# Gate projection with the frames' tiles standing and 24 weight columns moving, and moved products, loads and orders, in a hybrid GLA, mLSTM and ConvFFN step

## The reference, cut to what matters

```python
h = _rmsnorm(x, norm1)
gq, gk, gv, gr, glr, mq, mk, mv, mo, mi, mf = _split_proj(h @ w_in)
log_a = jax.nn.log_sigmoid((glr @ w_gla_a + b_gla_a).astype(f32)) / GLA_TAU
i_pre = mi.astype(f32) + b_m_i.astype(f32)
log_f = jax.nn.log_sigmoid(mf.astype(f32) + b_m_f.astype(f32))
o_g, S_new = _gla(...)          # gq, gk, gv, log_a;  gated by gr
h_m, C_new, n_new, m_new = _mlstm(...)   # mq, mk, mv, i_pre, log_f;  gated by mo
x = x + mix.astype(x.dtype) @ w_out
y, conv_new = _conv_ffn(_rmsnorm(x, norm2), conv_st, w_g, w_u, conv_w, conv_b, w_d)
```

## Time and profile before

| | us |
|---|---|
| median of 3 runs | 1443.26 (1441.57 to 1443.32) |
| profiled execution | 1442.54 |
| its span in the trace | 1440.7 |
| TensorE busy in the span | 1414.2 |

### The profile page before, as it was taken

How to read it: one execution, slowest core, us unless ns; L and a number is a source line. 1 busy time by engine, 2 the same in 40 slices (tenths; PEclk the granted TensorE clock), 3 DMA queues, 4 the chain that set the end, 5 groups by cost and what they waited for, 6 DMA issues and landing times.

```text
span 1440.7 us, 22509 instructions
## 1 busy us (share of the span) xinstructions
PE 1414.2 (98%) x8739; PEld 1293.3 (90%) x8739; DVE 601.2 (42%) x1234; ACT 418.7 (29%) x889; POOL 467.8 (32%) x452
## 2 busy tenths in 40 slices
PE   7999999999998999999999999999999999999997
PEld 7978888889997788898989999999999999999895
DVE  4453132466732455554243434333333333343436
ACT  6231232244322145741212222121212131303123
POOL 5121333467633244342222323231313131313210
PEclk9999999999999999999999999999999999999998
DMA  7123533334348473121010101010101011111003
GB/s 258 61 68 117 181 116 105 123 104 156 119 158 279 134 217 104 37 80 59 30 59 29 58 29 58 29 58 29 58 21 62 19 50 37 44 42 45 15 21 131
DMA packets 69473, 122.58 MB, mean 85 GB/s; under 512 B 5608, under 2 KB 41220, under 8 KB 68896
## 3 DMA queue, kind: packets, MB, share of 16 engines
q1 hardware_dynamic: 69263, 121.62, 25.2%
q10 hardware_dynamic: 144, 0.07, 0.0%
HBM read 93.02 MB, written 28.64 MB: 84 GB/s over the span
## 4 chain that ended last, share of the span: by engine, by line
PE 95%; DVE 1%; DMA 1%; ACT 1%; POOL 0%; SPq 0%; issue 0%; ACTq 0%; DVEq 0%; POOLq 0%
PE bank L93 29%; PE bank L95 29%; PE bank L94 29%; PE bank L1853 1%; PE bank L1066 1%; PE bank L993 1%; DMA m_og_b<-scratch_pN 1%; DVE m_x L2337 1%; PE bank L1123 1%; PE bank L1141 1%; PE bank L1806 0%; PE bank L1865 0%; PE bank L1836 0%; DVE m_x L2318 0%; PE bank L1835 0%; PE bank L1129 0%
## 5 line engine op out<-in xcount | busy, mean ns | idle before, releaser
L93 PE MATMUL bank<-f_h2T_hi,w_hi 128*128 128x384 f32 x1056 | 354.2, 335 | 0.0
L95 PE MATMUL bank<-f_h2T_hi,w_lo 128*128 128x384 f32 x1056 | 353.9, 335 | 0.0
L94 PE MATMUL bank<-f_h2T_lo,w_hi 128*128 128x384 f32 x1056 | 353.5, 335 | 0.0
L2138 POOL TENSOR_TENSOR f_a_lo<-f_gate_conv,f_a_hi 128x384 fp32r<-128x384 f32 x66 | 67.1, 1017 | 574.0 <-ACT f_a_hi L2187 574.0
L93 PEld LDWEIGHTS bank<-f_h2T_hi,w_hi 128*128 128x128 f32 x1056 | 198.3, 188 | 0.4
L94 PEld LDWEIGHTS bank<-f_h2T_lo,w_hi 128*128 128x128 f32 x1056 | 198.2, 188 | 0.4
L95 PEld LDWEIGHTS bank<-f_h2T_hi,w_lo 128*128 128x128 f32 x1056 | 198.2, 188 | 0.0
L2318 DVE TENSOR_TENSOR m_x<-bank,m_x 128x512 f32<-128x512 f32 x198 | 136.8, 691 | 126.1 <-PE bank L95 126.1
L93 PE MATMUL bank<-w_hi,f_a_hi 128*128 128x512 f32 x396 | 154.4, 390 | 0.4 <-DVE m_x L2318 0.2
L95 PE MATMUL bank<-w_hi,f_a_lo 128*128 128x512 f32 x396 | 154.3, 390 | 0.0
L94 PE MATMUL bank<-w_lo,f_a_hi 128*128 128x512 f32 x396 | 154.3, 390 | 0.0
(11 more groups left out here) (239 smaller groups left out, 2120.6 us busy)
## 6 DMA issues: line engine op xcount, KB each, us to landing
w_raw<-in_w SPq DMA_DIRECT2D x82, 512.0 KB, 3.6
f_raw<-in_w SPq DMA_DIRECT2D x21, 512.0 KB, 3.5
scratch_pN<-p_n_out SPq DMA_DIRECT2D x36, 256.0 KB, 2.1
scratch_pT<-p_t_out SPq DMA_DIRECT2D x36, 192.0 KB, 1.9
p_arena<-in_x SPq DMA_DIRECT2D x9, 512.0 KB, 6.5
p_arena<-scratch_pN SPq DMA_DIRECT2D x18, 256.0 KB, 3.2
m_x<-in_x SPq DMA_DIRECT2D x9, 512.0 KB, 6.5
m_t_in<-scratch_pT SPq DMA_DIRECT2D x9, 512.0 KB, 6.6
```

Of the source, the lines that this page charges most:

```text
L93: pe.matmul(out, stat[0], mov[0], start=start, stop=False)
L94: pe.matmul(out, stat[0], mov[1], start=False, stop=False)
L95: return pe.matmul(out, stat[1], mov[0], start=False, stop=stop)
L2138: pool.tensor_tensor(a_lo[q][:, s], gc[:, n % 2, :], a_hi[q][:, s].bitcast(F32), ALU.subtract).then_inc(a_split, 1)
```

## The change

The gate weights keep 24 columns: 4 forget, 16 rank, 4 input. High and low lie side by side, 48 columns for each of the 8 slices. A gate unit takes each of its three frame tiles as the standing operand: for each slice the high frames with 48 moving columns, then the low frames with the 24 high columns. VectorE's new `add_parts` adds the two halves and lays the rows out, rank columns three times, in a cleared buffer; `flip_gate` transposes three such tiles back, and ScalarE and VectorE read that as they read the gate unit before. In the front's list the gates move (gates 0 and 1 ahead of tile(0, 1), gate 2 right behind turn 2), the z products come a tile earlier, the logarithms right behind weight split 6. The last unit's product leaves the front's list on TensorE and ScalarE and is made in the back, behind the first two `turn_a`. SP loads the third og tile right behind the first tiles of the back. In the back's list `("scaled", 3)` and `("ffn", 0)` move behind the last but one `turn_b`.

```diff
-    order = [("sums", 0), ("w", 0), ("w", 1), ("turn", 0, 0), tile(0, 0), ("w", 2), ("sums", 1), tile(1, 0), tile(2, 0),
-             ("w", 3), ("scale", 1), ("turn", 1, 0), tile(3, 0), ("w", 4), ("turn", 1, 1), ("sums", 2), ("scale", 2), gate(0),
-             gate(1), ("turn", 2, 0), tile(0, 1), ("turn", 2, 1), ("w", 5)]
-    order += [tile(t, 1) for t in range(1, 4)] + [gate(2), ("ranks",), tile(0, 2)]
-    order += [("z", 0, rb) for rb in range(RB)] + [tile(1, 2)] + [("z", 1, rb) for rb in range(RB)] + [("logs",)]
-    order += [tile(2, 2), tile(3, 2)]
+    order = [("sums", 0), ("w", 0), ("w", 1), ("turn", 0, 0), tile(0, 0), ("places",), ("w", 2), ("sums", 1), tile(1, 0),
+             tile(2, 0), ("w", 3), ("scale", 1), ("turn", 1, 0), tile(3, 0), ("w", 4), ("turn", 1, 1), ("sums", 2), ("scale", 2),
+             gate(0), gate(1), tile(0, 1), ("flip_gate", 0), ("flip_gate", 1), ("turn", 2, 0), tile(1, 1), ("turn", 2, 1), ("w", 5)]
+    order += [gate(2), tile(2, 1), ("flip_gate", 2), ("ranks",), tile(3, 1)] + [("z", 0, rb) for rb in range(RB)] + [tile(0, 2)]
+    order += [("z", 1, rb) for rb in range(RB)] + [("logs",)] + [tile(t, 2) for t in range(1, 4)]
...
+    out.remove(("logs",))
+    out.insert(out.index(("w", N_UNITS_W)) + 1, ("logs",))
...
+    GATES = 2 * H + RANK
+    gate_w = w_hi[:, GATE_UNIT, 0:KD * 2 * GATES].rearrange("p (k m) -> p k m", m=2 * GATES)
+    gate_rows, low_parts = carve(0, [P, RT, P], [P, RT, GATES])
+
     def gate_parts(y):
 
-        dst = y[:, GATE_UNIT, :].rearrange("p (k m) -> p k m", m=P)
+        dst = gate_w[:, :, GATES * y:GATES * (y + 1)]
         src = raw[:, G_AT % 2, :].rearrange("p (k m) -> p k m", m=P)
-        rank = src[:, :, 64:64 + RANK]
-        for r in (slice(0, H), slice(H + RANK, 32 + H), slice(32 + H + RANK, P)):
-            yield dst[:, :, r], src[:, :, r]
-        for at in RANK_AT[0:2]:
-            yield dst[:, :, at:at + RANK], rank
+        for at, r in ((0, slice(0, H)), (H, slice(64, 64 + RANK)), (H + RANK, slice(32, 32 + H))):
+            yield dst[:, :, at:at + r.stop - r.start], src[:, :, r]
...
+        def last_product(pe):
+
+            i, = pieces_of(LAST_UNIT)
+            pe.wait_ge(taken[ring.before(LAST_UNIT)[0]], ring.before(LAST_UNIT)[1])
+            pe.wait_ge(g["piece_split"], i + 1)
+            for k in range(KD):
+                w = [y[:, i % NS_, k * P:(k + 1) * P] for y in (w_hi, w_lo)]
+                h = [y[:, k, LAST_UNIT[2] * RBW:(LAST_UNIT[2] + 1) * RBW] for y in hT]
+                mm = mm3(pe, ring.bank(LAST_UNIT)[:, 0:RBW], w, h, k == 0, k == KD - 1)
+            mm.then_inc(g["filled"], 1)
...
                 Done.attention(sp)
                 Done.row_block_stored(sp, M_STEPS[0] // JR)
                 early.load_tiles(sp, a, mem_m, 0)
+                Done.attention_rows(sp)
+                sp.dma_start(mem_m["og_b"][:, 0, :], a["pN"][2, M_STEPS[2]]).then_inc(early.og_in[2], 16)
...
+        def gate(x, rb):
+
+            out = enter(x)
+            if rb == 0:
+                pe.wait_ge(g["piece_split"], G_AT + 1)
+            pe.wait_ge(g["lo_done"], KD * (rb + 1))
+            for j in range(JR):
+                at = j * 2 * GATES
+                s = slice((rb * JR + j) * P, (rb * JR + j + 1) * P)
+                for k in range(KD):
+                    pe.matmul(out[:, at:at + 2 * GATES], hT[0][:, k, s], gate_w[:, k, :], start=k == 0, stop=False,
+                              skip_group_check=True)
+                    mm = pe.matmul(out[:, at:at + GATES], hT[1][:, k, s], gate_w[:, k, 0:GATES], start=False,
+                                   stop=k == KD - 1, skip_group_check=True)
+            mm.then_inc(g["filled"], 1)
+
+        def flip_gate(x, rb):
+            out = enter(x)
+            wait_taken(pe, ("gate", 0, rb))
+            for j in range(JR):
+                t = pe.transpose(out[:, j * P:(j + 1) * P], gate_rows[:, rb * JR + j, :], ident)
+            t.then_inc(g["filled"], 1)
...
+            low = low_parts[:, rb * JR:(rb + 1) * JR, :]
+            chain.link(dve.tensor_copy(low, parts[:, :, 1, :]))
+            for at, m in ((0, slice(0, H + RANK)), (32, inputs), (RANK_AT[1], rank), (RANK_AT[2], rank)):
+                u = dve.tensor_tensor(gate_rows[:, rb * JR:(rb + 1) * JR, at:at + m.stop - m.start], parts[:, :, 0, m],
+                                      low[:, :, m], ALU.add)
+            u.then_inc(taken["dve"], 1)
...
-    order = [("turn_a", 0), ("turn_a", 1), ("load", 0), ("load", 1), ("mask", 0)] + take(2) + [("rows", 0), ("qk", 0)] + take(2)
+    order = [("turn_a", 0), ("turn_a", 1), ("last", 0), ("load", 0), ("load", 1), ("mask", 0)] + take(2) + [("rows", 0), ("qk", 0)] + take(2)
...
-        order += [("turn_b", s - 1)] if s == RT - 1 else []
+        order += [("turn_b", s - 1), ("scaled", 3), ("ffn", 0)] if s == RT - 1 else []
...
-        order += {7: [("turn_n", 0, 1), ("scaled", 3), ("ffn", 0)], 8: [("scaled", 5)]}.get(s, [])
+        order += {7: [("turn_n", 0, 1)], 8: [("scaled", 5)]}.get(s, [])
```

More of the change, by code:

```diff
@@ L445, in front_entries @@
         second = second or x[:2] == ("n", 1)
-        if x[0] in ("gate", "z", "cols", "flip"):
+        if x[0] in ("gate", "flip_gate", "z", "cols", "flip"):
             out.append((x, "dve"))
@@ L521, in front @@
     N_AT = [x for x in order if x[0] == "n"]
+    LAST_UNIT = T_AT[-1]
+    assert order.index(LAST_UNIT) == max(order.index(u) for u in T_AT + N_AT)
     t_slot = lambda x: (T_AT.index(x) % 4, T_AT.index(x) // 4)
@@ L595, in products, with last_taken @@
             eng.wait_ge(g["filled"], len(ring.owner))
+        def last_product(pe):
[7 more added lines that the diff above has]
+            mm.then_inc(g["filled"], 1)
+        def last_taken(act):
+            slot, before = t_slot(LAST_UNIT)
+            act.wait_ge(g["filled"], ring.filled(LAST_UNIT))
+            act.wait_ge(t_stored[slot], 16 * before)
+            act.activation(tout[:, slot, :], ring.bank(LAST_UNIT)[:, 0:RBW], ACT.Copy).then_inc(taken["act"], 1)
         def scores(eng):
@@ L766, in lo @@
             if i == G_AT:
-                for (dst, src), (hi, _) in zip(gate_parts(w_lo), gate_parts(w_hi)):
+                for (dst, src), (hi, _) in zip(gate_parts(1), gate_parts(0)):
                     u = pool.tensor_tensor(dst, src, hi.bitcast(F32), ALU.subtract)
@@ L835, in _ @@
                 lower_exponents(x[1])
+            elif x[0] == "places":
+                pool.wait_ge(g["turned"], KD)
+                pool.memset(gate_rows, 0.0).then_inc(g["wa_zeroed"], 1)
     @block.scalar
@@ L843, in hi @@
             if i == G_AT:
-                for dst, src in gate_parts(w_hi):
+                for dst, src in gate_parts(0):
                     c = act.activation(dst, src, ACT.Copy)
@@ L924, in _ @@
                 act.activation(wa_parts[:, :], wa[:, :], ACT.Copy).then_inc(g["wa_hi"], 1)
-            elif name == "gate":
-                rb = x[2]
+            elif name == "flip_gate":
+                rb = x[1]
                 act.wait_ge(g["filled"], ring.filled(x))
@@ L965, in _ @@
                    .then_inc(taken["act"], 1)
-            elif name == "t" and ring.taken(x)[0] == "act":
+            elif name == "t" and ring.taken(x)[0] == "act" and x != LAST_UNIT:
                 slot, before = t_slot(x)
@@ L1149, in _ @@
                 turn(x[1], x[2])
-            elif name in ("gate", "t"):
+            elif name == "t" and x != LAST_UNIT:
                 tile(x, x[2])
+            elif name == "gate":
+                gate(x, x[2])
+            elif name == "flip_gate":
+                flip_gate(x, x[1])
             elif name == "z":
@@ L1155, in _ @@
                     pe.wait_ge(g["wa_split"], 1)
-                    wait_taken(pe, ("gate", 0, RB - 1))
+                    wait_taken(pe, ("flip_gate", RB - 1))
                 out = enter(x)
@@ L1200, in turn_lo, with add_parts @@
                                          op0=ALU.mult, op1=ALU.subtract).then_inc(g["lo_done"], 1)
+        def add_parts(x):
+            rb = x[2]
+            if rb == 0:
+                dve.wait_ge(g["wa_zeroed"], 2)
+            dve.wait_ge(g["filled"], ring.filled(x))
+            parts = ring.bank(x)[:, 0:JR * 2 * GATES].rearrange("p (j y m) -> p j y m", y=2, m=GATES)
+            rank, inputs = slice(H, H + RANK), slice(H + RANK, GATES)
+            low = low_parts[:, rb * JR:(rb + 1) * JR, :]
[4 more added lines that the diff above has]
+            u.then_inc(taken["dve"], 1)
         def gates(x):
-            rb = x[2]
+            rb = x[1]
             src = ring.bank(x)
@@ L1395, in _ @@
             elif name == "gate":
+                add_parts(x)
+            elif name == "flip_gate":
                 gates(x)
@@ L1580, in _ @@
         sp.dma_start(C_s[:, :, :, :], a["s_mc"]).then_inc(g["state_in"], 16)
-        done.attention_rows(sp)
-        load_og(2)
         sp.wait_ge(g["ones_set"], 1)
@@ L1760, in _ @@
```

(6 more changed lines are left out.)

## The result

The changed kernel takes 1456.43 us in the median of five runs (1452.73 to 1459.03), the kernel before 1443.26; the ratio is 1.0093, with a 95% interval of 1.0080 to 1.0105. The profiled execution of after took 1456.47 us, with a span of 1454.7. So the direction was foretold; the time lies 3.9 us over the predicted one and 0.9 us over the range.

The account below looks back on a forecast made before the run. TensorE, busy 98% of the span, was taken as the bound. Gates +3.3, turning back +1.3, wait +2.1, clock +13.7, logs -5.7, boundary -2.9, back -1.3 gave +10.5 on 1442.54: 1453.0, stated as 1452.5 us, range 1438 to 1455.5.

Parts of the forecast that it names:

- Logs: Earlier logarithms on ScalarE remove TensorE's 3.2 us low-half wait and 2.5 us of half clock: gain 5.7 us, 4 to 6.
- Boundary: Front to back: moved last unit and earlier og load remove the og wait and half-clock tail: gain 2.9 us, 1.5 to 4.
- back: Turn 7's split moved ahead of a scaled row and an ffn split shortens TensorE's row wait: gain 1.3 us, 0 to 1.5.
- the clock's term: Half clock in gates 0 and 1, gate 2 and the work behind them: 13.7 us lost, bounds 0 to 16.
- the moves win nothing at the boundary: Rival: front to back, key tiles, o_in rows or state load come later, so 2.9 us are missing; about 1455.5 us, chance 0.05.
- Gates: Narrow gate units: 144 products and loads at 0.11 us, 15.8 us in all, 3.3 us more than before.
- Clock in gates 0 and 1: 41 of 96 narrow products at full clock, 55 at half: 5.9 us lost, plus 2.1 us in dense work behind.
- Turning back: Nine transposes on TensorE, 1.0 us, and changes between transposes and products: 1.3 us more.
- the wait ahead of gate 2: TensorE waits for VectorE's low halves of the row block after turn 2: 2.1 us more, bounds 1.5 to 3.
- The clock holds: Rival: pause-free narrow gates keep full clock, so the 13.7 us loss is absent; 1439.3 us, chance 0.22.
- One place only: Rival: clock falls only at gate 2 with its wait, costing 5.7 us; gates 0 and 1 hold; about 1445 us, chance 0.13.
- Cheap narrow products: Rival: gate loads cost half of 0.11 us, gates gain 4.6 us at full clock; 1431 to 1437 us, chance 0.04.

Follow-up runs that it names:

- E7: Kernel before with z products a tile earlier, gate 2 behind tile(1, 1) and ScalarE's logarithms right behind weight split 6; 1438.63 us, ratio 0.9971.
- E2: Changed kernel with each narrow gate product moving its 48 weight columns three times on the same loads; 1446.94 us, ratio 1.0027.
- E6: Changed kernel with gate 2 behind tile(2, 1) in place of ahead of it; 1456.5 us, ratio 1.0094.
- E4: Changed kernel with one wait added: GpSimd's first weight split begins only after VectorE's three row scalings; 1452.57 us, ratio 1.0068.
- E8: Changed kernel without the moves of logarithms, last unit and og load, and back's order, z products still a tile earlier; 1462.53 us, ratio 1.0139.
- E5: Kernel before with only one wait added, GpSimd's first weight split after VectorE's three row scalings; 1440.2 us, ratio 0.9983.
- E1b: Kernel before with old wide gates, all the moves, and GpSimd's first split waiting for VectorE's row scalings; 1434.93 us, ratio 0.9944.
- E3: Changed kernel with the narrow gate products dealt among a tile's wide products, two and one in turn; median 1471.77 us, ratio 1.0207.

## Why the prediction was off

**The step that failed** is the pricing of the moves, 9.9 us in the sum and 6.5 in the runs in which they stand together (4.2 to 8.9). The waits were the right ones, and their sizes came from one execution. Logs, 5.7 in the sum: the half clock behind the wait for the low half was counted at 2.5 us from the one profile of five in which it lasted 6.8 us and not 3.4, and the wait was counted in full, where 1.1 of its 3.2 us stayed; the profiles show 3.3, E7's run 4.2 (2.5 to 6.1). Boundary, 2.9 in the sum: the og wait with its half clock was counted in full, where three of five profiles with the old order have no half clock there. Logs 3.3, boundary 1 to 3.3 and back 1.3 make 5.6 to 7.9 us, round the 6.5 measured. Beside this, 0.5 us were taken off the sum because the clock's term was thought to be rounded up, which it was not, and 0.7 us lie between the profiled execution and the median. The prediction took its range for "logs" (4 to 6) and "boundary" (1.5 to 4) from the same execution, so its upper end lay 0.9 us too low. The rival "the moves win nothing at the boundary" (1455.5) had nearly the right time by luck: the boundary did win, 2.3 us in its run (0.7 to 4.0), and nearly as much was missing from the logs.

**The base** had two errors that nearly cancel: no collision at the start (2.5 us less than is usual) and more half clock than is usual behind the two waits. So its 1442.54 us lies near the median by luck, and a sum made on it came out near the right place in each row of the first table and too low against the medians.

**Gates.** 144 products at 0.11 us: right to the hundredth; E2 shows that up to 144 columns do not change it.

**Clock in gates 0 and 1.** Forecast: 41 products at full clock, then 55 at twice the time. After kept 1.00 for 25 products (2.8 us), E6 for 25, E4 for 44 (4.9 us) and E8 for 52 (5.8 us): the 41 were a middle value. In the profile of after this is 1.5 us over the forecast (17.95 us against 8.40, +9.55; foretold 2.2 and 5.9), tile(0, 1) lost 2.55 us in place of 2.1, gate 2 and tile(2, 1) 6.1 in place of 6.8.

**Turning back, and the wait ahead of gate 2.** In after's timeline the six and three transposes take 0.65 and 0.25 us from start to start, 0.9 against 1.3, and the wait is 2.0 against 2.1. Both near. E6 shows that the wait is not to be had for nothing.

**Waits that were foretold.** Third row 0.2 us (under 0.4): right. Low half at the first n unit 1.1 us (under 0.5): the eighth half was not quite in time. Key tiles 2.0 us (1.3), and no wait for the o_in rows stands in the list (1 was foretold): the two together as foretold, in another place.

**Rivals.** "The clock holds" was put behind on the row that spoke against it, the light stretch at 259.3, and the clock did fall. That row was weaker than it looked: the same stretch kept 1.00 in six of the fourteen profiles. E2 shows the rival right for 144 columns in gates 0 and 1. "One place only" is E2. "Cheap narrow products" fell with the 0.11 us. The rule of the Trainium skill on the pace of pairs ("TensorE: Matmul & The Clock Gate", Back-to-back issue gap) gives 81 ns at 128 columns; the rows of E2 have 111 at 144.

## What to carry to other kernels

Count the weight loads, not the columns, when operands are swapped: a product that moves 24 columns past 128 standing ones took 0.11 us, as one with 144 did, and a run of products with 24 and 48 columns lost the clock although TensorE never paused, which cost more than the loads. Before pricing a wait and the half clock behind it from one profile, look at whether other profiles of the same part have them; a race for a port or a fall of the clock that is there in one execution may not be there in most. The moves without the new gates, with one wait that orders the start, are the version to keep: 1434.93 us, ratio 0.9944 (0.9930 to 0.9958).

## What was not expected of the hardware

- A stream of narrow products without a pause ran at the 1.2 GHz level for 15.2 us in after, and with four times the columns on the same loads at 2.4 GHz for 10.6 us.
- A 128 x 1024 scaling on VectorE took 2.83 us in place of 0.75 because GpSimd's split had begun 0.07 us ahead of it. In before the late third row tile turned the order round; one wait on GpSimd settled it in E4, E5 and E1b.
- The same program (E3) took 1454.2 or 1472 us, by whether the clock held in one mixed stream.
- Of five waits of TensorE for the same og tile, the two of 2.5 and 2.6 us had half clock behind them, and the three of 1.8 us had none.
